# Recurrent preparation for four chunks first with the level masks later, and stick-breaking scores one head at a time with exchanged keys loaded by SyncE

## The reference, cut to what matters

```python
# RWKV-7: per step, per head of 64 (8 heads)
w_log = -softplus(-(w0 + tanh(zw) @ w_decay_up)) - 0.5
decay = exp(-exp(w_log));  a = sigmoid(a0 + za @ w_iclr_up)
kk = (k * k_k).reshape(B, S, H, N);  kk = kk / max(norm(kk), 1e-12)
k = k * (1.0 + (a - 1.0) * k_a)
sa    = einsum('bhvk,bhk->bhv', state, -kk_t)
state = state * w_t[:, :, None, :] + sa[..., None] * (kk_t * a_t)[:, :, None, :] \
        + v_t[..., None] * k_t[:, :, None, :]
o_t   = einsum('bhvk,bhk->bhv', state, r_t)

# stick-breaking attention: 4 heads of 64, blocks of 128 queries
z = einsum('bhtd,bhsd->bhts', q_blk, k_blk) * scale
strict = s_pos < t_pos
log_beta = log_sigmoid(z);  log_1m_beta = where(strict, log_sigmoid(-z), 0.0)
between = cumsum(log_1m_beta, axis=3, reverse=True) - log_1m_beta
weights = where(strict, exp(log_beta + between), 0.0)
out = einsum('bhts,bhsv->bhtv', weights, v_blk)
```

## Time and profile before

| | before |
|---|---|
| median of three runs | 2454.03 us |
| the profiled execution | 2456.69 us |
| its span on the core | 2454.9 us |
| PE busy | 2363.5 us, 96% |
| DVE busy | 1389.8 us, 57% |
| ACT busy | 939.0 us, 38% |
| POOL busy | 1294.0 us, 53% |

### The profile page before, as it was taken

How to read it: one execution, slowest core, us unless ns; L and a number is a source line. 1 busy time by engine, 2 the same in 40 slices (tenths; PEclk the granted TensorE clock), 3 DMA queues, 4 the chain that set the end, 5 groups by cost and what they waited for, 6 DMA issues and landing times.

```text
span 2454.9 us, 45626 instructions
## 1 busy us (share of the span) xinstructions
PE 2363.5 (96%) x17622; PEld 1881.5 (77%) x17622; DVE 1389.8 (57%) x1747; ACT 939.0 (38%) x1418; POOL 1294.0 (53%) x768
## 2 busy tenths in 40 slices
PE   7999979999999999999999999999999999998798
PEld 5777769996877788888888877887877777773367
DVE  4377685556257666666665434564454366655464
ACT  3133352222335444444444212232252135557641
POOL 3332100001666677777777789789676445530045
PEclk9999999999999999999999999999999999999999
DMA  4311000000432333333332655465321111122033
GB/s 146 80 37 34 27 16 4 5 4 19 146 113 94 120 111 111 108 115 116 110 107 92 234 199 189 168 209 186 130 92 62 45 48 48 53 73 86 1 118 122
DMA packets 106616, 231.79 MB, mean 94 GB/s; under 512 B 7368, under 2 KB 46664, under 8 KB 106312
## 3 DMA queue, kind: packets, MB, share of 16 engines
q1 hardware_dynamic: 82496, 169.89, 20.8%
q10 hardware_dynamic: 23944, 59.46, 7.5%
HBM read 190.52 MB, written 38.80 MB: 93 GB/s over the span
## 4 chain that ended last, share of the span: by engine, by line
PE 73%; DVE 9%; ACT 6%; POOL 5%; issue 3%; DMA 3%; ACTq 0%; DVEq 0%; POOLq 0%; SPq 0%
PE ps L834 11%; PE ps L1310 6%; PE ps L1311 6%; PE ps L1312 6%; PE ps L1467 6%; PE ps L930 5%; PE ps L1439 4%; PE ps L1490 3%; PE ps L1348 2%; PE ps L1350 2%; PE ps L1351 2%; DMA w_raw<-wall 2%; POOL w_lo L621 2%; ACT ab L152 2%; POOL w_hi L618 2%
## 5 line engine op out<-in xcount | busy, mean ns | idle before, releaser
L618 POOL TENSOR_TENSOR w_hi<-w_raw,small 128x1024 fp32r<-128x1024 f32 x156 | 305.9, 1961 | 738.4 <-PE ps L834 274.6
L621 POOL TENSOR_TENSOR w_lo<-w_raw,w_hi 128x1024 fp32r<-128x1024 f32 x156 | 431.2, 2764 | 12.3
L683 POOL TENSOR_TENSOR slot_lo<-scr,slot_hi 128x512 fp32r<-128x512 f32 x116 | 160.6, 1395 | 85.5 <-ACT slot_hi L152 85.5
L834 PE MATMUL ps<-x_hi,w_hi 128*128 128x512 f32 x448 | 176.0, 402 | 5.3 <-POOL w_lo L621 2.3
L834 PE MATMUL ps<-x_lo,w_hi 128*128 128x512 f32 x448 | 172.1, 393 | 0.0
L834 PE MATMUL ps<-x_hi,w_lo 128*128 128x512 f32 x448 | 172.0, 393 | 0.0
L152 ACT ACTIVATE slot_hi<-scr 128x512 fp32r<-128x512 f32 x116 | 73.4, 633 | 195.6 <-POOL scr L693 77.7
L1310 PE MATMUL ps<-t_hi,slot_hi 128*128 128x512 f32 x348 | 135.5, 389 | 0.4 <-ACT p L152 0.4
L1311 PE MATMUL ps<-t_lo,slot_hi 128*128 128x512 f32 x348 | 135.4, 389 | 0.0
L1312 PE MATMUL ps<-t_hi,slot_lo 128*128 128x512 f32 x348 | 135.4, 389 | 0.0
L639 POOL COPY xx<-rmask 128x512 f32<-128x512 f32 x16 | 11.8, 749 | 227.5 <-PE ps L1133 174.6
(11 more groups left out here) (389 smaller groups left out, 6471.9 us busy)
## 6 DMA issues: line engine op xcount, KB each, us to landing
w_raw<-wall SPq DMA_DIRECT2D x191, 512.0 KB, 3.5
f_raw<-f_spill SPq DMA_DIRECT2D x62, 512.0 KB, 4.5
f_spill<-cg SPq DMA_DIRECT2D x30, 512.0 KB, 3.4
v_raw<-wall SPq DMA_DIRECT2D x29, 512.0 KB, 3.5
ada_w<-wada ACTq DMA_DIRECT2D x24, 512.0 KB, 3.9
fill_spill<-stage ACTq DMA_DIRECT2D x24, 256.0 KB, 2.0
x_in<-xT ACTq DMA_DIRECT2D x8, 512.0 KB, 8.8
x<-xT ACTq DMA_DIRECT2D x8, 512.0 KB, 4.2
```

The costliest lines, as they stand in the source:

```text
L618: nc.gpsimd.tensor_tensor(w_hi[:, u, :, :], w_raw[:, u, :, :], sm["one"].unsqueeze(2).to_broadcast([P, KT, P]), ALU.mult).then_inc(S("w_hi ...
L621: nc.gpsimd.tensor_tensor(w_lo[:, u, :, :], w_raw[:, u, :, :], w_hi[:, u, :, :].bitcast(F32), ALU.subtract).then_inc(S("w_split"), 1)
L683: tt_p(slot_lo[i][:, :, :], src, slot_hi[i][:, :, :].bitcast(F32), ALU.subtract).then_inc(later("s_lo")[0], 1)
L834: last = mm(ps[:, 2 * u + h, :], w[:, u, k, :], x[:, k, h * 512:(h + 1) * 512], start=(k == 0 and w is w_hi and x is hi), stop=(k == KT - ...
```

## The change

In the preparation, DVE multiplies only the first four chunks (256 positions) of `kka` for all four tiles and of the mixed key for tiles 2 and 3; the other 768 positions come at the end of its loop turns `n == -3` and `n == -2`. The copies of the level masks on ACT go from ahead of `key_mix(3)` to the end of turn -3, PE's transposes of them behind the last `spread` and into bank 5, and the waits for them into turn -1. ACT's gate sigmoid goes ahead of `rates(3)`.

In the stick-breaking attention the half `x` 0 of a head's queries now lies in the other head's partitions, so that for `b` < 4 the two halves of one head use the two halves of the rows. The keys for it are loaded a second time, exchanged, into `k_turn`, by four transfers on SyncE's queue ahead of the gates. The one transfer of queries and keys becomes five on ACT's queue. Scores are made by head, with one count of `sb_z` for each; where `z_ahead_head` allows it a head's scores stand ahead of `remainder(2m)`.

```diff
@@ SyncE
                     sp.wait_ge(S("o2_mm"), NB)
+                    sp.wait_ge(S("past_in"), 16)
+                    for p in range(2):
+                        for e in range(2):
+                            q = slice(64 * (1 - e), 64 * (1 - e) + 64)
+                            sp.dma_start(k_turn[p][q, :], fill_dram[2 + p][64 * e:64 * e + 64, 0:512]).then_inc(S("past_in"), 16)
                     for k in range(KT):
@@ TensorE
             for m in range(1, 4):
-                if m == 3:
-                    turned_masks()
                 pe.wait_ge(S("kkn_done"), m)
                 spread(sm["kinv"], m, 6).then_inc(S("kinv_bc"), 1)
                 if m < 3:
                     low_rank(m + 1)
+            turned_masks()
...
-            pe.wait_ge(*once("lmask_done"))
             for n in range(-2, N_CHUNK + 1):
+                if n == -1:
+                    pe.wait_ge(*once("lmask_done"))
...
+            def scores_of(n):
+                p, b = SB_STEPS[n // 2]
+                e = n % 2
+                if z_free_head(n):
+                    pe.wait_ge(S("sb_w"), z_free_head(n))
...
+                if b < 4:
+                    pe.wait_ge(S("hn_log"), 3 * (p + 1))
+                    pe.wait_ge(S("past_in"), 80)
                 for x, c, t in halves_of(b):
+                    g = e if x else 1 - e
+                    q = slice(64 * g, 64 * g + 64)
+                    keys = proj2[q, 11 + p, b * P:(b + 1) * P] if x else k_turn[p][q, b * P:(b + 1) * P]
+                    mm(z_out(n, x)[:, c:], keys, proj2[q, 9 + p, 512 * e + c:512 * e + 512],
+                       start=True, stop=True, skip_group_check=True)
...
+            def z_scores(heads):
+                for n in heads:
+                    scores_of(n)
+                for n in heads:
+                    mask_of(n)
...
             for m in range(len(SB_STEPS)):
-                if z_ahead(m + 1):
-                    z_scores(m + 1)
+                heads = [n for n in (2 * m + 2, 2 * m + 3) if n < 2 * len(SB_STEPS)]
+                z_scores([n for n in heads if z_ahead_head(n)])
                 remainder(2 * m)
                 if m:
                     weigh(m - 1)
-                if m + 1 < len(SB_STEPS) and not z_ahead(m + 1):
-                    z_scores(m + 1)
+                z_scores([n for n in heads if not z_ahead_head(n)])
                 remainder(2 * m + 1)
@@ ScalarE
             rates(2)
             key_mix(2)
+            fn(proj[:, 19, :], proj[:, 19, :], ACT.Sigmoid).then_inc(S("lora_act"), 1)
             rates(3)
-            fn(proj[:, 19, :], proj[:, 19, :], ACT.Sigmoid).then_inc(S("lora_act"), 1)
+            key_mix(3)
...
+                if n == -3:
+                    level_masks()
...
-                        act.dma_start(proj2[:, 9:13, :], fill_dram[0:4].rearrange("k p t -> p k t")).then_inc(landed("qk_back")[0], 16)
+                        act.dma_start(proj2[:, 11:13, :], fill_dram[2:4].rearrange("k p t -> p k t"))\
+                            .then_inc(landed("qk_back0")[0], 16)
+                        for g in range(2):
+                            for e in range(2):
+                                act.dma_start(proj2[64 * g:64 * g + 64, 9:11, hc(e)],
+                                              fill_dram[0:2][:, 64 * e:64 * e + 64, hc(int(g == e))].rearrange("k p t -> p k t"))\
+                                    .then_inc(landed(f"qk_back{1 + 2 * g + e}")[0], 16)
...
-                act.wait_ge(S("sb_z"), n // 2 + 1)
+                act.wait_ge(S("sb_z"), n + 1)
@@ VectorE
+            NEAR = 4 * RC
+            far = slice(NEAR, T)
...
-                tt(proj[:, 10 + m, :], proj[:, 10 + m, :], tt_[:, m % 2, :], ALU.mult)
+                mixed(m, slice(0, T if m < 2 else NEAR))
                 dve.wait_ge(S("kkn_done"), m + 1)
-                tt(kka[:, m, :], kka[:, m, :], kkn[:, m, :], ALU.mult)
+                scaled_keys(m, slice(0, NEAR))
...
-            dve.wait_ge(*once("lmask_done"))
             for n in range(-4, N_CHUNK + 1):
+                if n == -1:
+                    dve.wait_ge(*once("lmask_done"))
...
+                if n == -3:
+                    for m in (2, 3):
+                        mixed(m, far)
+                if n == -2:
+                    for m in range(4):
+                        scaled_keys(m, far)
```

More of the change, by code:

```diff
@@ L94 @@
     "in_a": ("bias_in", "rmask_in") + tuple(f"x_again{k}" for k in range(8)) + ("gmask_in", "sbmask_in"),
-    "in_b": ("smask_in", "smask2_in", "qk_back") + tuple(f"x2_back{k}" for k in range(8)),
+    "in_b": ("smask_in", "smask2_in") + tuple(f"qk_back{k}" for k in range(5)) + tuple(f"x2_back{k}" for k in range(8)),
 }
@@ L416, in z_free, with z_free_head, z_ahead_head @@
                        default=0)
+        def z_free_head(n):
+            return max([k + 1 for k in range(n) if set(z_banks(k)) & set(z_banks(n))], default=0)
+        def z_ahead_head(n):
+            return n < 2 * len(SB_STEPS) and z_free_head(n) <= 2 * (n // 2 - 1)
         def z_ahead(m):
```

44 lines of the change are left out of this document (21 added, 23 removed).

## The result

The changed kernel takes 2461.34 us (median of 9 executions, 2458.38 to 2464.41) and the kernel before, beside it, 2453.65 (9, 2449.43 to 2458.40): ratio 1.003, 95% interval 1.002 to 1.004. It is 7.7 us slower; I had forecast 2.4. Its profiled execution took 2461.82 us with a span of 2460.0. From 22 us to the last low-rank product at 326, far ahead of the change, its matmuls stand 1.1 to 1.2 us earlier than in the first profile of before, because the low clock fell elsewhere in the first projection (the first matmul starts at 10.32 and 10.30 us).

What follows compares the result with a forecast made beforehand. A chain over DVE and ACT was taken to set the recurrence's start, and PE to carry any shift to the end. Preparation 3.0, attention -0.7 and transfers 0.1 gave +2.4 us: 2456.4 us median, range 2449 to 2460.

Steps and rivals of the forecast that it cites:

- The sign of each part: Whole change: preparation slower by 3.0 us, attention faster by 0.7, transfers slower by 0.1.
- the mechanism up to the recurrence: Preparation: first `ar` earlier, second chunk's `m1` later behind wide DVE operations, then PE idle and its clock lower.
- the price of the preparation: Preparation: 1.7 us for the late second chunk plus 1.3 for PE's clock, 3.0 us in all.
- the cost of PE's clock: Preparation, behind PE's gap of 3.8 us at about 348 to 352: lower clock costs 1.3 us, 0 if it holds.
- Ahead of the loop: Preparation: six DVE operations shrink from 1.22 to 0.43 us, so `prepare_a(0)` starts 4.0 us earlier.
- Inside the loop: Preparation loop: 6.2 us of wide DVE operations ahead of the second chunk's `m1` make it 1.7 us late.
- The transfers: Query and key loads for the attention: four more issues and rows of 2 KB cost 0.1 us.
- The attention: Stick-breaking attention: worth -0.7 us, the middle between -0.1 and -1.4.
- rival (c): Attention: one head's two halves don't run side by side, so slower, 2463.5 us; chance 0.1.
- the end at -1.4: Attention, steps 4 and 12: the second head's score does not wait for the first, worth -1.4 us.
- The new wait: Attention, step 5: head 10's early score waits for an exponent and holds up PE; `soft(10)` 1.8 us later.
- Rival (a): Attention: ACT loses its mask waits at six steps, 12 us, giving 2445 us, or 2451 at half; chance 0.1.

Runs made afterwards that it cites:

- prep_only: The kernel before with the preparation part of the change alone, attention and transfers as before: 2462.3 us.
- pe_filled: The kernel before with the preparation part alone, plus 32 matmuls nobody reads in PE's idle stretch ahead of the level at turn -1: 2454.3 us.
- attn_only: The kernel before with the attention part and its transfers alone, preparation as before: 2451.4 us.
- after_filled: The changed kernel with 32 matmuls nobody reads on PE ahead of the level at turn -1: 2452.2 us.
- both_warm: both_mended with 32 matmuls nobody reads on PE behind the last `kkn`, ahead of the first chunk's products: 2453.1 us.
- both_mended: The changed kernel with `kka` of later chunks made chunk by chunk, in place of four operations on 768 columns: 2450.7 us.

## Why the prediction was wrong

The sign of each part and the mechanism up to the recurrence were right. What failed is the price of the preparation: 3.0 us forecast, 6.1 in prep_only's profile and 8.6 by its median. The step that failed most is the cost of PE's clock, which I took at 1.3 us and let end at the first level; the runs show 2.2 there and 1.6 more at 583 to 608. Term by term:

- **Ahead of the loop** I had the first `ar` 4.0 us earlier; it was 3.4, as POOL's copies still stretched two operations of 256 columns (0.86 and 0.68 for 0.42).
- **Inside the loop** "1.7 us late" measured 2.2: `m` at 349.83 + 1.2. This is the same 0.6 us once more, not a second miss: the counting inside the loop was sound, and pe_filled isolates the lateness (2.3 with the clock held).
- **"I take 1.3 us for the gap of 3.8"** measured 2.2 (prep_only less pe_filled). The gap was about right (4.11), the rate too; I charged the group behind it and a few tenths, from the earlier trace rows, but six groups, from L1113 at 351.37 to L1100 at 355.66, ran slow, and all were on the path.
- **Missing: the clock beyond the change.** I ended its cost at the level. At 583 to 608 the same matmuls took 1.6 us more than before, in both profiles of the change and in prep_only.
- **The transfers** 0.1, measured about 0.5, by a wait that I did not name. The scores did not wait; the fill's stage did:
```profile
2200.91 2.63 ACTq L2388 DMA_DIRECT2D proj<-fill_spill  x4
...
2211.84 0.60 ACT L152 ACTIVATE stage<-ps 128x512 f32<-128x512 f32 x1 [5.62 <-DMA fill_spill<-stage]
```
A write issued at 2206.30 had to land before the stage could be used again. It landed 5.5 us after its issue, which stood behind the 2 MB on the same queue, where the other two writes of this line took 2.0; in before that write took 4.3 and ACT waited for PE instead. The stage follows the first score 0.6 us later, where it was 0.1. The four issues took 2.63 us, not the 1.5 that I charged.
- **The attention** -0.7, measured -2.9 where both profiles have one fall of the clock (attn_only and before's second), some -2.2 with two in each, and no gain with four in each; the median of attn_only says -2.2, with an interval from -5.6 to +2.7. I took the middle between a second score that waits and one that does not; it does not (the step-4 pair took 1.28 us to its mask, 2237.53 to 2238.81, for 1.29 before), so rival (c) is out, and the end at -1.4 was the one. The new wait was real: PE idle 2.50 for an exponent ahead of head 10's score, `soft(10)` 0.7 late where I had 1.8. That the clock falls behind it in four of six profiles, with `soft(10)` then 2.2 us late or more, I did not have; so `soft(16)` is 1.2 us early in the changed kernel's first profile and 0.3 late in its second. Beyond the -1.4 about 1 us is again the clock: the means of squares that took 3.17 us in the earlier trace rows (2.81 in before's second profile) take 1.94 in both profiles of the change. It is no property of the change, for they take 3.63 in after_filled and 3.41 in both_warm. Rival (a), 12 us, failed as argued: remainders took the place of the masks.

The measured terms are 2.2 + 2.2 + 1.6 + 0.5 - 2.9 = +3.6, or +4.3 with -2.2 for the attention. The medians say +6.6 to +7.7, with intervals that begin at 2.2 and 4.9. Part of the rest is the preparation's (prep_only: 6.1 by its stretches, 8.6 by the median, interval 5.2 to 12). It stays unlocated: what is left lies in untouched stretches, where each profile puts its few us of low clock elsewhere.

The Trainium skill, TensorEngine Tiling (Array Packing), Key Properties, has each change of tiling mode drain TensorE. No price of such a drain can be told apart here: a lone head's score group took 1.06 us to its mask, and the pair of heads 1.28. (The 0.2 us that the prediction has beyond a group's columns is 0.3 by its own figures, 1.13 less 4 x 0.21; the sum didn't use it.)

The Trainium skill, DMA: Bandwidth & Descriptors, gives 512 bytes as the least for line rate, so rows of 2 KB should cost nothing. The transfers did get slower, but they don't test this rule alone: the 2 MB took five slices of 1.88 us with 395, 320, 227, 239 and 105 GB/s, and four before with 310, 419, 413 and 145, where all rows were of 4 KB. First the changed kernel, 2193 to 2268, then before, 2185 to 2260, in 40 slices:
```profile
GB/s 0 0 140 0 50 395 320 227 239 105 0 140 0 0 169 222 358 389 411 419 413 419 282 2 9 0 4 0 0 0 0 0 0 0 0 0 0 0 0 0
```
```profile
GB/s 0 0 140 0 48 310 419 413 145 1 32 108 0 31 323 332 382 402 415 419 419 81 0 0 9 0 4 0 0 0 0 0 0 0 0 0 0 0 0 0
```
Three things changed at once: the rows, the spacing of the four issues (0.66 us each), and that each of the four transfers writes only 64 of the 128 partitions. No run separates them, so the price of the rows isn't shown.

## What to carry to other kernels

Work that is split off to be done "later" has to be put where its engine has slack, piece by piece: four operations in one place undid what six shorter ones had won, while the same work in twelve pieces kept 1.7 us of it. An idle stretch of TensorE can cost more than its length (here 2.2 us more for 4.1 idle): add the lower clock behind it, over everything on the path that it touches, and ask where the low clock will land before filling or moving a gap. A score, or any early work, that itself waits must not stand ahead of work that another engine is waiting for. And when the clock falls a different number of times in two profiles, a stretch of one can't be compared with that of the other before the falls are counted.

## What the runs showed of the hardware that I had not expected

- All 126 executions of the kernel before in these runs lie between 2445 and 2460 us, and the mean granted clock tells most of it (correlation -0.93): 0.001 more clock is 2.1 us less. The change's second set had a mean of 0.9826, after_filled's 0.9858, and the means of their times are 7.3 us apart.
- 32 matmuls that do nothing made the changed kernel 8 us faster, and put at another place, 15 us earlier, both_mended 2.4 us slower by the medians (1.0 by the means).
- Identical matmuls 230 us behind an edit ran at a mean of 0.92, 0.96 or 1.00 of full clock, depending on the kernel, and the same in both profiles of the two kernels that were profiled twice.
